# Modulation steps at equal distances, columns prepared a turn ahead and y summed in place in the mixer turns of a two-layer trunk

## The chip, the cores and the metric

The kernel runs on one core of a Trainium2 chip. The metric is the device time of one execution in microseconds (us); smaller is better. The core has TensorE (PE; its weight loads are shown apart as PEld), VectorE (DVE), ScalarE (ACT), GpSimd (POOL) and SyncE (SP), which issues most transfers.

## What is computed

The reference is one inference step of a diffusion trunk with two layers, for 512 latent and 128 context tokens of width 1024, in float32. The change lies in layer 0, whose mixer runs a state-space scan (16 heads, forwards and backwards) beside a gated convolution:

```python
def mixer_ssd_conv(h, P, e, h0):
    u = h @ P['ssd_w_in'][e]
    z, xbc, dt_raw, bg, cg, xin = jnp.split(u, [s1, s2, s3, s4, s5], axis=-1)
    y_a, states = ssd_mixer(z, xbc, dt_raw, ...)
    y_b = bg * dwconv(cg * xin, P['sc_conv_w'][e])
    return jnp.concatenate([y_a, y_b], axis=-1) @ P['mix0_w_out'][e], states

# in ssd_mixer, after the two scans:
    y = y_f + flip(y_b) + xs * jnp.sum(d_skip.astype(jnp.float32), axis=0)[:, None]
    y = y.reshape(b, l, SSD_INNER) * jax.nn.silu(z.astype(jnp.float32))

# in run_stream, for each layer:
    m = jax.nn.silu(cvec) @ P['ada_w'][i] + P['ada_b'][i]
```

The last line gives the modulation (shift, scale and gate of each of the 12 sections of 1024 columns). The kernel computes most of it during the mixer, section by section.

## The kernel before

Features lie on the 128 partitions, tokens along the free dimension: an activation chunk is 128 features by T = 644 columns (128 context, 4 of padding, 512 latent). Each float32 product is made of three: high by high, low by high and high by low, with weights split on the core. SyncE loads a weight block of 128 columns into `raw` (two buffers), ScalarE copies it to `w_hi` (`split`, L1092), GpSimd subtracts that from `raw` into `w_lo` (`low`, L550), and PE uses the pair from a ring of four slots.

The mixer makes eight turns, one for each pair of heads (j = 0 to 7), in two groups of four; `mixer_pair` holds PE's part of a turn. A turn has four products with weights (z, cg, xin, bg), each in two halves of four chunks (`gemm_half(s, h)`: lines L613, L614, L617, 24 products of 322 columns). The small products of the scan are written by hand between these halves: transposes of the pair's input `xsj`, rows of decays in bank 5 (`rows_of`), states, y and the context state. The second half of the last product and the first half of the next turn's first product stand at the turn's end, in that order. Engines meet by counting semaphores; every queue keeps the order of the program.

One turn also makes one modulation section in four steps (`section(0)` to `section(3)`, `ada_step`, L684: four products of 512 columns). Each step needs 1 MB of `ada_w` in the one buffer `ada`. SyncE may load a step only when PE has used the one before (`ada_used`), and SyncE's queue holds, in this order per turn: step 0, `raw` slots 0 and 1 of the next turn, step 1, slot 2, step 2, slot 3, step 3. A `raw` load waits until GpSimd has finished the slot two before it:

```python
sp.wait_ge(S["low_split"], b + s - RAW + 1 + 4 * i)     # weights(): a raw buffer is free
sp.wait_ge(S["ada_used"], step)                         # ada_load()
for s in ((0, 1), (2,), (3,), ())[q]: following(s)      # raw loads behind step q
```

On VectorE a turn begins with three copies: the pair's input to `xsj`, and the pair's columns of two tables to `pick` and `col` (L1706 to L1711); `prep_ready` then lets PE and ScalarE begin. It goes on with weighted inputs, differences of decays (`seg`, L1738), the states `hin` (L1756, waited for by PE before L844), the convolution (`gpad`, L1791; `cgs`, L1647 and L1648), y (L1797 to L1802: a sum into `xsj`, a product with the gate into `xs`), the second half of the mixer's output (`yb`, L1806) and, last, the modulation's columns (L1694), which it reads from the same bank 4 into which the next turn's transposes go. ScalarE makes exponentials, gates and splits; its order in a turn begins with the exponential of rows 0, that of `seg` 0, the gate `zs` of the finished first product, the exponential of rows 1 (`cs`, L1226), that of `seg` 1, and the split of the next turn's slot 0.

Of the kernel before, what the change touches and what calls it, by code (L numbers as in the profile page):

```python
# [20 lines left out]
ALU = mybir.AluOpType  # L21
ACT = mybir.ActivationFunctionType

P = 128
# [17 lines left out]
DR, DC = 15, 31  # L42
TABW = 64
BIG = 1e30
MIX_STEPS = 11
FF = 2816
FC = FF // P
FA = 12
# [81 lines left out]
def trunk(nc, x_prompt, x_sample, state_ssd, cache_k, cache_v, c, c_ctx, ada_w, ada_b, norm_mix_g, norm_ffn_g,  # L130
# [6 lines left out]
    with ExitStack() as ctx:  # L137
# [461 lines left out]
        def _(pe):  # L599
# [185 lines left out]
            def rows_of(u):  # L785

                lhs = pick[:, u % 2, u // 2:u // 2 + 1].broadcast_to([P, P])
                for b in range(2):
                    mm = t.matmul(ps[:, 5, 2 * b * P:2 * b * P + 2 * P], lhs, sum_rows[b][:], start=True, stop=True)
                mm.then_inc(S["rows_ready"], 1)  # L790

            def mixer_pair(j0, i, more=True):


                base = SLOT_MIX + 4 * j0

                def gemm_half(s, h, i=i):
                    if h == 0:
                        pe.wait_ge(S["low_split"], base + s + 1 + 4 * i)
                        tile_free(TILE_MIX + 4 * j0, 4, i, s)  # L800
                    mm = half_slot(s % 2, s % RING, range(4 * h, 4 * h + 4), act_hi, act_lo, h == 0, h == 1)
                    if h == 1:
                        mm.then_inc(S["slot_used"], 1)

                def section(q):

                    ada_step(7, ADA_STEPS * (j0 + i) + q, q)

                def bank5_free(n):
                    pe.wait_ge(S["seg_ready"], 5 * (j0 + i) + n)  # L810

                if i is None:
                    gemm_half(0, 0, 0)
                    return
                pe.wait_ge(S["prep_ready"], j0 + i + 1)
                for n in range(LC):
                    mm = t.transpose(ps[:, 4, n * P:n * P + P], xsj[:, LAT0 + n * P:LAT0 + n * P + P], ident[:])
                mm.then_inc(S["xtok_ready"], 1)
                rows_of(0)
                gemm_half(0, 1)  # L820
                section(0)
                bank5_free(1)
                rows_of(1)
                pe.wait_ge(S["xtok_taken"], j0 + i + 1)
                t.transpose(ps[:, 4, 0:P], xsj[:, 0:NCTX], ident[:])
                pe.wait_ge(S["h0_loaded"], 16 * (j0 + i) + 16)
                t.transpose(ps[:, 4, P:2 * P], h0[:, 0, :], ident[:])
                t.transpose(ps[:, 4, 2 * P:3 * P], h0[:, 1, :], ident[:]).then_inc(S["ctok_ready"], 1)
                gemm_half(1, 0)
                bank5_free(2)  # L830
                rows_of(2)

                pe.wait_ge(S["ctok_taken"], j0 + i + 1)
                for n in range(LC - 1):
                    mm = t.matmul(ps[:, 4, n * P:n * P + P], btok[:, n, :], xdw[:, 2, n, :], start=True, stop=True)
                mm.then_inc(S["hf_ready"], 1)
                gemm_half(1, 1)
                section(1)
                bank5_free(3)
                rows_of(3)  # L840

                pe.wait_ge(S["hf_taken"], j0 + i + 1)
                for n in range(LC - 1):
                    mm = t.matmul(ps[:, 4, n * P:n * P + P], btok[:, n + 1, :], xdw[:, 3, n + 1, :], start=True, stop=True)  # L844
                mm.then_inc(S["hb_ready"], 1)
                gemm_half(2, 0)
                bank5_free(4)

                for h in range(2):
                    for r in range(2):  # L850
                        lhs = col[:, LC * KINDS + K_DA, r, h:h + 1].broadcast_to([P, P])
                        mm = t.matmul(ps[:, 5, (2 * h + r) * P:(2 * h + r + 1) * P], lhs, tri[:, r, :], start=True, stop=True)
                mm.then_inc(S["rows_ready"], 1)
                gemm_half(2, 1)

                section(2)
                gemm_half(3, 0)
                section(3)

                pe.wait_ge(S["m_ready"], 3 * (j0 + i) + 2)  # L860
                pe.wait_ge(S["hb_taken"], j0 + i + 1)
                for n in range(LC):
                    cols = slice(n * P, n * P + P)
                    for r in range(4):
                        for h in range(2):
                            hc = slice(64 * h, 64 * h + 64)
                            lhs = xdw[:, r, n, hc] if r < 2 else hin[:, r - 2, n, hc]
                            rhs = mbuf[:, 2 * h + r, cols] if r < 2 else cs[:, 2 * h + r - 2, cols]
                            mm = t.matmul(ps[64 * h:64 * h + 64, 6, cols], lhs, rhs, start=(r == 0), stop=(r == 3))
                mm.then_inc(S["y_ready"], 1)  # L870
                pe.wait_ge(S["row_copied"], j0 + i + 1)
                ada_columns(4, 3 * P)

                pe.wait_ge(S["m_ready"], 3 * (j0 + i) + 3)
                for r in range(2):
                    t.matmul(ps[:, 4, r * P:r * P + P], xdw[:, 2 + r, LC, :], btok[:, LC, :], start=True, stop=True)
                for r in range(2):
                    for h in range(2):
                        mm = t.matmul(ps[64 * h:64 * h + 64, 4, 2 * P:3 * P], xdw[:, r, LC, 64 * h:64 * h + 64],
                                      mbuf[:, 4, (2 * h + r) * P:(2 * h + r + 1) * P], start=(r == 0), stop=(r == 1))  # L880
                mm.then_inc(S["cstate_ready"], 1)
                gemm_half(3, 1)
                if more:
                    gemm_half(0, 0, i + 1)
# [562 lines left out]
        def _(dve):  # L1447
# [242 lines left out]
            def modulation(m0, cols):  # L1690

                adab = par[:, bass.ds(R_ADAB + m0, C)].rearrange("p (b n) -> p b n", b=2).unsqueeze(3).broadcast_to([P, 2, C // 2, 2])
                dst = mod[:].rearrange("p m c s -> p (m c) s")[:, bass.ds(m0, C), :].rearrange("p (b n) s -> p b n s", b=2)
                tt(dst, cols.rearrange("p (n b s) -> p b n s", n=C // 2, b=2), adab, ALU.add).then_inc(S["mod_ready"], 1)  # L1694


            for g in range(GROUPS):
# [1 line left out]
                    group_taken(g)  # L1699
                j0 = (C // GROUPS) * g  # L1700
                tb = TILE_MIX + 4 * j0
                with st.loop(C // GROUPS, MIX_STEPS) as i:
                    j = j0 + i

                    st.wait()
                    st.did(v.tensor_copy(xsj[:], xs[:, bass.ds(j * T, T)]))  # L1706
                    mine = unit[:, bass.ds(2 * j, HEADS + 2)]
                    v.tensor_copy(pick[:], bass.AP(tensor=mine.tensor, offset=mine.offset, ap=[mine.ap[0], [HEADS, 2], [1, 2]]))
                    scv = sc[:].rearrange("p n k u -> p (n k u)")[:, bass.ds(2 * j, NC * KINDS * 32 - 14)]
                    pair = bass.AP(tensor=scv.tensor, offset=scv.offset, ap=[scv.ap[0], [32, NC * KINDS], [HEADS, 2], [1, 2]])  # L1710
                    v.tensor_copy(col[:], pair).then_inc(S["prep_ready"], 1)  # L1711
                    dve.wait_ge(S["prep_ready"], j + 1)
                    colv = col[:].rearrange("p (n k) r h -> p n k r h", k=KINDS)

# [69 lines left out]
                    for r in range(2):  # L1784
                        rl = slice(r * P, r * P + P)
                        ins = tt(m4[:, :, rl], m4[:, :, rl], bcast(gm[:, r, ctx_cols], 1, [P, 2, P]), ALU.mult)
                    ins.then_inc(S["m_ready"], 1)

                    dve.wait_ge(S["slot_used"], SLOT_MIX + 3 + 4 * j)
                    dve.wait_ge(S["tile_free1"], tb // 2 + 1 + 2 * i)  # L1790
# [3 lines left out]

                    dve.wait_ge(S["y_ready"], j + 1)
                    skip = dskip[:, bass.ds(j, 1)]
                    st.then_wait(stt(xsj[:, LAT0:T], xsj[:, LAT0:T], skip, ps[:, 6, :], ALU.mult, ALU.add))  # L1797
                    st.did(stt(xs[:, bass.ds(j * T + LAT0, NLAT)], xsj[:, LAT0:T], 0.5, zs[:, LAT0:T], ALU.mult, ALU.mult))
                    dve.wait_ge(S["cstate_ready"], j + 1)
                    v.tensor_copy(sto[:].rearrange("p r n -> p (r n)"), ps[:, 4, 0:2 * P]).then_inc(S["cstate_taken"], 1)  # L1800
                    st.then_wait(stt(xsj[:, 0:NCTX], xsj[:, 0:NCTX], skip, ps[:, 4, 2 * P:3 * P], ALU.mult, ALU.add))
                    st.did(stt(xs[:, bass.ds(j * T, NCTX)], xsj[:, 0:NCTX], 0.5, zs[:, 0:NCTX], ALU.mult, ALU.mult))  # L1802
                    st.wait()
                    dve.sem_inc(S["ya_ready"], 1)
                    dve.wait_ge(S["slot_used"], SLOT_MIX + 4 + 4 * j)
                    tt(F(yb[:, bass.ds(j * T, T)]), V(1), F(cgs[:]), ALU.mult).then_inc(S["tile_free1"], 1)  # L1806
                    add_squares(1, j)

                    dve.wait_ge(S["mod_turned"], j + 1)
                    modulation((2 + j) * C, ps[:, 4, 3 * P:3 * P + 2 * C])  # L1810

            inverse(1)
            with dve.Fori(0, C) as i:
# [280 lines left out]
```

## Time and profile before

| what | value |
|---|---|
| median of the runs shown | 2083.84 us (2082.85 to 2084.32, 3 runs) |
| the profiled execution | 2088.62 us |
| its span, first to last instruction | 2086.8 us |
| busy: PE, PEld, DVE, ACT, POOL | 94%, 90%, 50%, 33%, 31% of the span |
| mean granted clock of TensorE | 0.973 of full speed |
| the eight mixer turns | about 196 to 592 us of the span |

The busy share of PE is an average over stages; matmuls are pipelined and their ends are modelled, so 94% does not say that PE is at its peak for 94% of the time. Idle time of an engine matters only where another waits for it.

### The profile page before, as it was taken

The page shows a single profiled execution, that of the slowest core. Times are in us where ns is not written, and L with a number is a line of the kernel's source. Part 1 is how long each engine was busy: PE and PEld are TensorE (multiplying, and loading weights), DVE is VectorE, ACT ScalarE, POOL GpSimd, SP SyncE. Part 2 cuts the span into 40 slices and gives each one's busy share as a digit, 9 for nine tenths or more (in the row PEclk, how much of TensorE's full clock was granted, in tenths as well). Part 3 has the DMA queues.
Part 4 walks back from the last instruction along what each step waited for, and adds up shares of the span by engine and source line. Part 5 has one row for each costly group of instructions (what it writes and reads, how often), then busy time and mean ns, then how long its engine had stood idle before and what let it go on. Part 6 is the DMA issues. An engine that isn't in the chain of part 4 may idle for free. (4 is left out here: it accounts for less than half of the span.)

```text
span 2086.8 us, 36378 instructions
## 1 busy us (share of the span) xinstructions
PE 1971.2 (94%) x13563; PEld 1887.0 (90%) x13563; DVE 1042.2 (50%) x1987; ACT 687.4 (33%) x1043; POOL 637.7 (31%) x314
## 2 busy tenths in 40 slices
PE   6699999899999899999999988989999999999997
PEld 3498888787889899999999988989998999999997
DVE  3544776666661365521555334656635655125543
ACT  1433222222231244422323422127724434223333
POOL 0322222222223233344334522332212333433342
PEclk9899999999999999999999999999999999999998
DMA  8123444344444222223222341221031222232222
GB/s 290 41 58 89 145 145 144 120 135 148 129 166 145 81 64 71 70 69 90 71 70 57 97 136 52 71 56 29 19 132 43 80 80 58 75 89 70 65 64 73
DMA packets 280040, 192.31 MB, mean 92 GB/s; under 512 B 25370, under 2 KB 267414, under 8 KB 279462
## 3 DMA queue, kind: packets, MB, share of 16 engines
q1 hardware_dynamic: 276950, 185.61, 29.7%
q10 hardware_dynamic: 3024, 5.78, 0.7%
q8 instruction: 46, 0.75, 0.2%
q14 instruction: 20, 0.16, 0.0%
HBM read 181.31 MB, written 10.06 MB: 92 GB/s over the span
## 5 line engine op out<-in xcount | busy, mean ns | idle before, releaser
L550 POOL TENSOR_TENSOR w_lo<-raw,w_hi 128x1024 fp32r<-128x1024 f32 x244 | 591.7, 2426 | 1344.5 <-ACT w_hi L1092 1344.5
L613 PE MATMUL ps<-act_hi,w_hi 128*128 128x322 f32 x2752 | 850.6, 316 | 13.6 <-DVE act_lo L1554 11.6
L614 PE MATMUL ps<-act_lo,w_hi 128*128 128x322 f32 x2624 | 806.3, 313 | 0.0
L617 PE MATMUL ps<-act_hi,w_lo 128*128 128x322 f32 x2752 | 637.2, 313 | 0.0
L613 PEld LDWEIGHTS ps<-act_hi,w_hi 128*128 128x128 f32 x2752 | 528.2, 192 | 26.4 <-issue 16.4
L614 PEld LDWEIGHTS ps<-act_lo,w_hi 128*128 128x128 f32 x2624 | 501.4, 191 | 0.0
L617 PEld LDWEIGHTS ps<-act_hi,w_lo 128*128 128x128 f32 x2752 | 468.2, 190 | 0.0
L1092 ACT ACTIVATE w_hi<-raw 128x1024 fp32r<-128x1024 f32 x244 | 256.4, 1052 | 452.5 <-PE ps L617 400.0
L613 PE MATMUL ps<-f_hi,w_hi 128*128 128x322 f32 x704 | 214.2, 311 | 0.0
L614 PE MATMUL ps<-f_lo,w_hi 128*128 128x322 f32 x704 | 213.7, 310 | 0.0
L1827 DVE SCALAR_TENSOR_TENSOR x<-ps,mod,x 128x128 f32 (+1 forms) x144 | 54.4, 433 | 262.5 <-PE ps L617 262.0
L617 PE MATMUL ps<-f_hi,w_lo 128*128 128x322 f32 x704 | 161.9, 311 | 0.0
L613 PEld LDWEIGHTS ps<-f_hi,w_hi 128*128 128x128 f32 x704 | 133.5, 190 | 0.0
L614 PEld LDWEIGHTS ps<-f_lo,w_hi 128*128 128x128 f32 x704 | 132.8, 189 | 0.0
L1648 DVE SCALAR_TENSOR_TENSOR ft<-fg,par,ft 128x644 f32<-128x644 f32 x44 | 124.3, 2824 | 6.8 <-DVE ft L1647 6.5
L617 PEld LDWEIGHTS ps<-f_hi,w_lo 128*128 128x128 f32 x704 | 118.0, 188 | 0.0
L1863 DVE TENSOR_TENSOR fg<-ps,spread 128x644 f32<-128x644 f32 x44 | 36.5, 830 | 130.8 <-PE ps L617 122.1
L1339 ACT ACTIVATE fe<-ft,gb 128x130 f32<-128x130 f32 x88 | 44.9, 557 | 127.1 <-DVE ft L1648 127.1
L1482 DVE TENSOR_TENSOR acc<-acc,sq 128x644 f32<-128x644 f32 x48 | 65.6, 1367 | 28.1 <-ACT sq L1103 27.7
L1335 ACT ACTIVATE ft<-fg,par 128x644 f32<-128x644 f32 x44 | 36.7, 834 | 127.4 <-DVE fg L1863 127.3
L1647 DVE SCALAR_TENSOR_TENSOR ft<-fg,par,ft 128x644 f32<-128x644 f32 x44 | 43.3, 984 | 44.1 <-ACT ft L1335 43.6
L1343 ACT ACTIVATE f_hi<-fa 128x644 f32 x44 | 32.7, 743 | 95.1 <-DVE fa L1875 95.1
(294 smaller groups left out, 2173.2 us busy)
## 6 DMA issues: line engine op xcount, KB each, us to landing
ada<-in_ada_w SPq DMA_DIRECT2D x40, 1024.0 KB, 5.3
raw<-in_ssd_w_in SPq DMA_DIRECT2D x44, 512.0 KB, 3.9
raw<-in_ffn_w_gate SPq DMA_DIRECT2D x44, 512.0 KB, 3.8
raw<-in_ffn_w_up SPq DMA_DIRECT2D x44, 512.0 KB, 3.8
raw<-in_ffn_w_down SPq DMA_DIRECT2D x32, 384.0 KB, 3.4
raw<-in_na_w_qkv SPq DMA_DIRECT2D x24, 512.0 KB, 3.7
raw<-in_ffn_w_down SPq DMA_DIRECT2D x32, 320.0 KB, 3.2
first<-in_ada_w SPq DMA_DIRECT2D x8, 1024.0 KB, 12.1
```

Source lines behind the costliest of these rows:

```text
L550: g.tensor_tensor(w_lo[:, s], raw[:, s % RAW], w_hi[:, s], ALU.subtract).then_inc(S["low_split"], 1)
L613: t.matmul(out, hi, chunk_of(src_hi, k0 + k, cols), start=start, stop=False)
L614: t.matmul(out, hi, chunk_of(src_lo, k0 + k, cols), start=False, stop=False)
L617: mm = t.matmul(ps[:, 2 * tset + h, 0:HALF], lo, chunk_of(src_hi, k0 + k, cols), start=False, stop=stop)
L1092: a(w_hi[:, s], raw[:, s % RAW], ACT.Copy).then_inc(S["high_split"], 1)
L1335: a(ft[k][:], fg[k][:, 1:T + 1], ACT.Copy, scale=w1).then_inc(S["ffn_mid"], 1)
L1339: ins = a(fe[k][:, lo:hi], ft[k][:, lo:hi], ACT.Gelu_apprx_tanh, bias=gb[:, k, stream:stream + 1])
L1482: tt(acc[:], acc[:], sq[:], ALU.add).then_inc(S["squares_used"], 1)
L1647: st.then_wait(stt(dst[:], buf[:, 0:T], w[:, bass.ds(w0, 1)], dst[:], ALU.mult, ALU.add))
L1648: return stt(dst[:], buf[:, 2:T + 2], w[:, bass.ds(w2, 1)], dst[:], ALU.mult, ALU.add)
L1827: ins = stt(dst, ps[:, 2 * k + bank, lo:hi], gate, dst, ALU.mult, ALU.add)
L1863: tt(F(fg[k][:, 1:T + 1]), V(0), F(spread[:]), ALU.mult).then_inc(S["tile_free0"], 1)
```

## The change

There are five edits, all in the mixer's turns. PE's `section(0)`, `section(1)` and `section(2)` each move ahead of a half-product (sections 1 and 2 past further small products). VectorE's three copies become a function `prepare`, called once ahead of the first turn and then inside each turn, for the next one, just before the product into `gpad`; the last turn of the second group is written out behind its loop, without it. The modulation's columns move ahead of `yb`. PE waits for them (`mod_ready`) before the next turn's transposes, since VectorE no longer makes the copies behind them. y is summed and gated in `xs` itself, so that `xsj` is free early, and a step count goes from 11 to 10.

```diff
-MIX_STEPS = 11
+MIX_STEPS = 10
...
+                pe.wait_ge(S["mod_ready"], j0 + i + 1)
                 pe.wait_ge(S["prep_ready"], j0 + i + 1)
...
                 rows_of(0)
+                section(0)
                 gemm_half(0, 1)
-                section(0)
                 bank5_free(1)
...
                 gemm_half(1, 0)
+                section(1)
                 bank5_free(2)
...
                 gemm_half(1, 1)
-                section(1)
                 bank5_free(3)
...
                 gemm_half(2, 0)
+                section(2)
                 bank5_free(4)
...
                 gemm_half(2, 1)
-
-                section(2)
                 gemm_half(3, 0)
                 section(3)
...
-                    st.wait()
-                    st.did(v.tensor_copy(xsj[:], xs[:, bass.ds(j * T, T)]))
+                def prepare(j):
+
+                    if not (isinstance(j, int) and j == 0):
+                        dve.wait_ge(S["ctok_ready"], j)
+                    v.tensor_copy(xsj[:], xs[:, bass.ds(j * T, T)])
...
                     v.tensor_copy(col[:], pair).then_inc(S["prep_ready"], 1)
...
                     ins.then_inc(S["m_ready"], 1)
+                    if more:
+                        prepare(j + 1)
 
                     dve.wait_ge(S["slot_used"], SLOT_MIX + 3 + 4 * j)
...
-                    st.then_wait(stt(xsj[:, LAT0:T], xsj[:, LAT0:T], skip, ps[:, 6, :], ALU.mult, ALU.add))
+                    lat, ctx_ = xs[:, bass.ds(j * T + LAT0, NLAT)], xs[:, bass.ds(j * T, NCTX)]
+                    st.then_wait(stt(lat, lat, skip, ps[:, 6, :], ALU.mult, ALU.add))
+                    st.did(stt(lat, lat, 0.5, zs[:, LAT0:T], ALU.mult, ALU.mult))
...
                     dve.sem_inc(S["ya_ready"], 1)
+                    dve.wait_ge(S["mod_turned"], j + 1)
+                    modulation((2 + j) * C, ps[:, 4, 3 * P:3 * P + 2 * C])
                     dve.wait_ge(S["slot_used"], SLOT_MIX + 4 + 4 * j)
                     tt(F(yb[:, bass.ds(j * T, T)]), V(1), F(cgs[:]), ALU.mult).then_inc(S["tile_free1"], 1)
                     add_squares(1, j)
 
-                    dve.wait_ge(S["mod_turned"], j + 1)
-                    modulation((2 + j) * C, ps[:, 4, 3 * P:3 * P + 2 * C])
+                if g == 0:
+                    prepare(0)
+                loops = C // GROUPS - g
+                with st.loop(loops, MIX_STEPS) as i:
+                    pair_of_heads(i)
+                if g > 0:
+                    pair_of_heads(loops, more=False)
```

PE's order at the start of a turn, before and then after. `xsj` is the pair's input, `pick` the columns of `rows_of`, `ada` the modulation's weights, `act` and `w` the operands of a half-product.

```order
L817 MATMUL ps<-ident,xsj 128x128 x4
L789 MATMUL ps<-sum_rows_98,pick 128x256
L789 MATMUL ps<-sum_rows_99,pick 128x256
L613 MATMUL ps<-act_hi,w_hi 128x322
L614 MATMUL ps<-act_lo,w_hi 128x322
```
```order
L818 MATMUL ps<-ident,xsj 128x128 x4
L789 MATMUL ps<-sum_rows_98,pick 128x256
L789 MATMUL ps<-sum_rows_99,pick 128x256
L680 ISA
L684 MATMUL ps<-ada,csil_w 32x512 x4
L613 MATMUL ps<-act_hi,w_hi 128x322
L614 MATMUL ps<-act_lo,w_hi 128x322
```

The four products of section 0 (L684) now stand ahead of the half-product instead of behind it; its line of the transposes is L818 now.

PE's order at the end of `gemm_half(2, 0)`, before and then after. `tri,col` is the last product into bank 5.

```order
L617 MATMUL ps<-act_hi,w_lo 128x322 x2
L810 REGISTER_ALU
L852 MATMUL ps<-tri,col 128x128 x4
L613 MATMUL ps<-act_hi,w_hi 128x322
L614 MATMUL ps<-act_lo,w_hi 128x322
L613 MATMUL ps<-act_hi,w_hi 128x322
```
```order
L617 MATMUL ps<-act_hi,w_lo 128x322 x2
L680 ISA
L684 MATMUL ps<-ada,csil_w 32x512 x4
L810 REGISTER_ALU
L854 MATMUL ps<-tri,col 128x128 x4
L613 MATMUL ps<-act_hi,w_hi 128x322
L614 MATMUL ps<-act_lo,w_hi 128x322
L613 MATMUL ps<-act_hi,w_hi 128x322
```

Section 2 now stands ahead of the `tri` products; before, it stood behind them and the half-product that follows.

VectorE's order in mid-turn, before and then after: the last products of the decays (`mbuf`), then the product into `gpad`.

```order
L1786 TENSOR_TENSOR mbuf<-mbuf,gm 128x2x128 x2
L1789 REGISTER_ALU
L1790 REGISTER_ALU
L1791 TENSOR_TENSOR gpad<-ps,cgs 128x644
L1647 ISA
L1647 SCALAR_TENSOR_TENSOR cgs<-gpad,par,cgs 128x644
```
```order
L1789 TENSOR_TENSOR mbuf<-mbuf,gm 128x2x128 x2
L1706 ISA
L1706 COPY xsj<-xs 128x644
L1708 ISA
L1708 COPY pick<-unit 128x4
L1711 REGISTER_ALU
L1711 COPY col<-sc 128x100
L1794 REGISTER_ALU
L1795 ISA
L1796 TENSOR_TENSOR gpad<-ps,cgs 128x644
L1647 ISA
L1647 SCALAR_TENSOR_TENSOR cgs<-gpad,par,cgs 128x644
```

The three copies for the next turn now stand between the last product with `gm` and the product into `gpad`.

## Rows read from the trace of the kernel before

**Rows 1.** Waits of TensorE by line and releaser, window 196 to 592 us.

```profile
PE ps L684 <- DMA ada<-in_ada_w: 14.9, 8, 2.4
PE ps L817 <- DVE col L1711: 14.2, 8, 4.6
PE ps L844 <- DVE hin L1756: 2.2, 8, 0.3
```

**Rows 2.** Timeline of PE in one turn: start, length, line, operation, idle before.

```profile
247.97 0.66 PE L817 MATMUL ps<-ident,xsj 128*128 128x128 f32 x4 [0.97 <-DVE col L1711]
...
252.34 1.07 PE L684 MATMUL ps<-ada,csil_w 128*32 128x512 f32 x8
...
263.93 0.94 PE L844 MATMUL ps<-xdw,btok 128*128 128x128 f32 x6 [0.28 <-DVE hin L1756]
...
268.26 1.05 PE L852 MATMUL ps<-tri,col 128*128 128x128 f32 x8
...
272.80 1.07 PE L684 MATMUL ps<-ada,csil_w 128*32 128x512 f32 x8
...
279.41 1.06 PE L684 MATMUL ps<-ada,csil_w 128*32 128x512 f32 x8 [1.81 <-DMA ada<-in_ada_w]
...
280.41 0.66 PE L869 MATMUL ps<-mbuf,xdw 128*64 128x128 f32 x8
...
294.54 0.66 PE L817 MATMUL ps<-ident,xsj 128*128 128x128 f32 x4 [0.97 <-DVE col L1711]
```

**Rows 3.** Busy time by stretch and engine, granted clock (third from the end).

```profile
326.00:332.50 6.50, 6.42 (x73) 5.41 (x74) 0.00 (x0) 0.60 (x1) 0.00 (x0) 0.74 0.62 196
521.00:527.00 6.00, 6.00 (x72) 5.14 (x64) 0.00 (x0) 0.60 (x1) 0.00 (x0) 0.72 0.63 203
569.00:575.50 6.50, 5.82 (x66) 4.31 (x68) 0.00 (x0) 0.60 (x1) 0.00 (x0) 0.74 0.44 141
```

**Rows 4.** Timeline of SyncE's queue, 172 to 300 us.

```profile
177.05 7.51 SPq L353 DMA_DIRECT2D raw<-in_ssd_w_in  x2
184.60 0.58 SPq L418 DMA_DIRECT2D ada<-in_ada_w  x1
...
260.32 0.37 SPq L353 DMA_DIRECT2D raw<-in_ssd_w_in  x1
...
274.07 0.37 SPq L418 DMA_DIRECT2D ada<-in_ada_w  x1
```

**Rows 5.** The page's DMA issues: count, KB each, median us to landing.

```profile
ada<-in_ada_w SPq DMA_DIRECT2D x40, 1024.0 KB, 5.3
raw<-in_ssd_w_in SPq DMA_DIRECT2D x44, 512.0 KB, 3.9
```

**Rows 6.** The tile `ada`, issues from 184 to 186 us (one).

```profile
DMA to landing us min/median/max: 6.1/6.1/6.1
```

**Rows 7.** Timeline of ACT in the same turn as rows 2.

```profile
253.08 0.69 ACT L1236 ACTIVATE zs<-ps 128x644 f32<-128x644 f32 x1
253.88 0.60 ACT L1226 ACTIVATE cs<-ps 128x512 f32<-128x512 f32 x1
```

**Rows 8.** Timeline of PE: first turn of each of the two groups.

```profile
198.97 1.12 PE L817 MATMUL ps<-ident,xsj 128*128 128x128 f32 x4 [4.60 <-DVE col L1711]
...
393.84 1.11 PE L817 MATMUL ps<-ident,xsj 128*128 128x128 f32 x4 [3.74 <-DVE col L1711]
```

**Rows 9.** Timeline of DVE: the turn of rows 2, then the group change.

```profile
273.00 0.83 DVE L1791 TENSOR_TENSOR gpad<-ps,cgs 128x644 f32<-128x644 f32 x1 [0.66 <-PE ps L617]
...
284.33 0.75 DVE L1797 SCALAR_TENSOR_TENSOR xsj<-xsj,dskip,ps 128x512 f32<-128x512 f32 x1 [5.43 <-PE ps L869]
...
291.69 2.60 DVE L1706 COPY xsj<-xs 128x644 f32 x1
...
392.98 0.50 DVE L1706 COPY xsj<-xs 128x644 f32 x1 [0.35 <-DVE btok L1673]
```

**Rows 10.** Timeline of POOL, 285 to 296 us.

```profile
291.18 2.77 POOL L550 TENSOR_TENSOR w_lo<-raw,w_hi 128x1024 fp32r<-128x1024 f32 x1 [12.96 <-ACT w_hi L1092]
```

More of the change, by code:

```diff
@@ L1701, in _ @@
                 tb = TILE_MIX + 4 * j0
-                with st.loop(C // GROUPS, MIX_STEPS) as i:
-                    j = j0 + i
-                    st.wait()
-                    st.did(v.tensor_copy(xsj[:], xs[:, bass.ds(j * T, T)]))
+                def prepare(j):
+                    if not (isinstance(j, int) and j == 0):
+                        dve.wait_ge(S["ctok_ready"], j)
+                    v.tensor_copy(xsj[:], xs[:, bass.ds(j * T, T)])
                     mine = unit[:, bass.ds(2 * j, HEADS + 2)]
@@ L1711, in _, with pair_of_heads @@
                     v.tensor_copy(col[:], pair).then_inc(S["prep_ready"], 1)
+                def pair_of_heads(i, more=True):
+                    j = j0 + i
                     dve.wait_ge(S["prep_ready"], j + 1)
@@ L1796, in _ @@
                     skip = dskip[:, bass.ds(j, 1)]
-                    st.then_wait(stt(xsj[:, LAT0:T], xsj[:, LAT0:T], skip, ps[:, 6, :], ALU.mult, ALU.add))
-                    st.did(stt(xs[:, bass.ds(j * T + LAT0, NLAT)], xsj[:, LAT0:T], 0.5, zs[:, LAT0:T], ALU.mult, ALU.mult))
+                    lat, ctx_ = xs[:, bass.ds(j * T + LAT0, NLAT)], xs[:, bass.ds(j * T, NCTX)]
+                    st.then_wait(stt(lat, lat, skip, ps[:, 6, :], ALU.mult, ALU.add))
+                    st.did(stt(lat, lat, 0.5, zs[:, LAT0:T], ALU.mult, ALU.mult))
                     dve.wait_ge(S["cstate_ready"], j + 1)
                     v.tensor_copy(sto[:].rearrange("p r n -> p (r n)"), ps[:, 4, 0:2 * P]).then_inc(S["cstate_taken"], 1)
-                    st.then_wait(stt(xsj[:, 0:NCTX], xsj[:, 0:NCTX], skip, ps[:, 4, 2 * P:3 * P], ALU.mult, ALU.add))
-                    st.did(stt(xs[:, bass.ds(j * T, NCTX)], xsj[:, 0:NCTX], 0.5, zs[:, 0:NCTX], ALU.mult, ALU.mult))
+                    st.then_wait(stt(ctx_, ctx_, skip, ps[:, 4, 2 * P:3 * P], ALU.mult, ALU.add))
+                    st.did(stt(ctx_, ctx_, 0.5, zs[:, 0:NCTX], ALU.mult, ALU.mult))
                     st.wait()
                     dve.sem_inc(S["ya_ready"], 1)
+                    dve.wait_ge(S["mod_turned"], j + 1)
+                    modulation((2 + j) * C, ps[:, 4, 3 * P:3 * P + 2 * C])
                     dve.wait_ge(S["slot_used"], SLOT_MIX + 4 + 4 * j)
```

## Prediction

> **What bounds the kernel now.** I read the waits of TensorE first, over the eight mixer turns (196 to 592 us of a span of 2086.8). Two waits matter: 14.9 us in eight pieces for the transfer into `ada`, and 14.2 us in eight pieces for `col`, the last copy that VectorE makes ahead of a turn; a third, 2.2 us for `hin`, is small [rows 1]. Then the timeline of one turn, PE alone, shows where they stand. A turn begins with the transposes of `xsj` (I call that moment T0, here 247.97). Its four modulation sections (L684) start at 252.34, one not shown, 272.80 and 279.41: the last two are 6.6 us apart, and the fourth stands 1.81 us idle. After the y product and two half-products the next transposes stand 0.97 us idle [rows 2]. Outside these, PE goes from one product to the next, so in these turns PE is the bound and each of its idle stretches is on the path.
>
> Third, the granted clock. In the turn of rows 2 y ran at full clock (its first eight products take 0.66 us); so it did in four others. In three of the eight turns the stretch around y shows a granted clock of 0.74, 0.72 and 0.74 [rows 3], a mix of the levels 2.4 and 1.2 GHz. Ahead of y PE had in every turn stood idle for the `ada` wait, 2.4 us in the longest [rows 1]. The loss is 6.5 x 0.26 + 6.0 x 0.28 + 6.5 x 0.26 = 5.1 us.
>
> The profiled execution took 2088.62 us, of which 2086.8 is the span; that is 4.8 above the median of the runs, 2083.84. I make the sum against the profiled execution and take the same difference off the median. About 0.2% of it, 4 us, is what a measurement can tell from no change.
>
> **Sections moved up.** Sections 0, 1 and 2 each change places with a half-product. A half takes 3.5 to 3.8 us: 272.80 - 268.26 less 1.05 for the `tri` products gives 3.5, and 279.41 - 1.81 - 272.80 less 1.00 for the section's own products (279.41 to 280.41) gives 3.8 [rows 2]. After the change at least two halves lie between any section and the next, so sections start 8 us or more apart (1.0 + 2 x 3.5). What must fit between them: the section's own 1.0, the SyncE issue 0.2 behind its last product (272.80 + 1.07 to 274.07 [rows 2, 4]), and 5.3 us to land [rows 5]: 6.5 us. So the wait before section 3 goes: -14.9 us. PE does the same products as before.
>
> The tight place is section 2. SyncE's queue issues the load for it behind `raw` of slot 2 of the next turn, and that issue waits for GpSimd's low part, not for PE: 260.32, which is T0 + 12.35 [rows 4]. Section 2 will stand where the `tri` products stand now, T0 + 20.29 [rows 2]. In the one place where an `ada` load stood right behind a `raw` load (the second of the pair at 177.05 ends at 184.56 and is issued 0.37 before that, `ada` at 184.60), it landed after 6.1 us instead of 5.3 [rows 4 to 6]. So it is issued at T0 + 12.8 to 13.2 and lands at 18.9 to 19.3: 1.0 to 1.4 us to spare, and I cost this wait at 0. The bound from the other side lets the two transfers pass one after the other whole: 12.35 + 3.9 + 5.3 = 21.55 [rows 5], 1.3 us too late, 8 x 1.3 = 10 us.
>
> A rule of the Trainium skill speaks for that bound: the page DMA: Bandwidth & Descriptors, section Queues, rings and completion order, says that each DMA engine takes the descriptors of one ring in order, so `ada` stands behind the whole `raw` load. The trace agrees that it is later, by 0.8 us and not by the 3.9 of a whole load; by the page's order alone with whole loads the gain would be 10 us less.
>
> **ScalarE behind section 0.** ScalarE's gate (`zs`) needs the first product whole, and that now ends 1.0 us later. Today `zs` runs at 253.08, when the product has been done since 252.34, and the exponential of the second rows (`cs`) follows at 253.88 [rows 7]. With the product's end at about 253.4, `zs` starts at about 253.5 and `cs` at about 254.2, 0.3 later. VectorE's chain to `hin` hangs on `cs`, and PE waits for `hin` already (0.28 [rows 2]), so this is on the path: +0.3 x 8 = 2.4 us. Bounds: 0, and the whole of section 0, 8 us. SyncE's issue and section 2 both shift by it, so the margin above stays.
>
> **Columns prepared in mid-turn.** The copies to `xsj`, `pick` and `col` go to the place before the `gpad` product. Six of the eight starts lose 0.97 each: -5.8. The first start, 4.60, keeps its wait: the copies still follow the last input block there. At the change of groups, 3.74, PE also waits for the new scores; only the copies go, with 0.35 of idle time ahead: 393.84 - 392.98 + 0.35 = 1.2 [rows 8, 9]. Together -7.0 us. After the change the new scores (`btok`) are what is late there.
>
> What the copies cost at the new place: 0.50 us for the large one when GpSimd is idle (392.98), 2.60 when GpSimd runs its low part (291.18 to 293.95, and the copy ends at 294.29 [rows 9, 10]). GpSimd's low part of slot 2 starts only behind `gpad` (its split follows ScalarE's scaling of `gpad`), and that of slot 1 is by then done, so I take 0.9 for the three. VectorE idles 0.66 there now and section 2 delays both it and PE alike, so `gpad` comes at most 0.3 late. Cover behind it: VectorE idles 5.43 us before y [rows 9], of which 1.81 (the removed wait) and 1.0 (section 2 ahead of it) go, and 2.6 is left. Even the 2.60 copy would fit; without the cover the modulation would come late, and PE needs that only at the next turn, two halves later. So: 0.
>
> **Modulation ahead of `yb`, y in place.** PE's new wait at a turn's start is for the modulation, and PE's whole turn is queued behind it, so every engine would wait with it. Its products are done before PE begins the last two halves (7 us), and VectorE has it right behind y, so this wait is 0. y in place changes operands, not counts: 0. The extra copy of the last turn's code runs straight on: 0.
>
> **Clock.** With no idle stretch before y, I take the three drops as gone: -5.1. Bounds: 0 if they stay, 3.4 more gain or loss if the slow stretch behind each of the two long starts (198.97, 393.84 [rows 8]) ends one turn's worth (1.7, as each drop above) earlier or later.
>
> **Sum.** -14.9 - 5.8 - 1.2 - 5.1 + 2.4 = -24.6. Profiled execution 2064.0, runs 2083.84 - 24.6 = 2059.2.
>
> **Rivals.**
> The wait goes to section 2. For: the load is issued late by GpSimd's pace and meets `raw`. Against: 6.1 us, not 9. It costs 0 to 10 us, at most 2069. Chance 0.15.
> The clock drops stay, as the narrow y products follow section 3 as before. For: they happen in y. Against: five turns with the same y had none. 2064.3. Chance 0.15.
> The change doesn't do what it says: section 3 still waits, since its load is queued behind `raw` of slot 3. Against: that is issued before section 2 ends. Only the turn starts gain: 2083.84 - 7.0 + 2.4 = 2079.2. Chance 0.05.
> Slower. The place is the same load of section 2: SyncE can't issue it before GpSimd's low part of the next turn's slot 0, which waits for ScalarE's split behind `cs`. If that chain slipped as section 0 moved, each turn would wait at section 2. It decides against the change above 24.6 / 8 = 3.1 us a turn, which is an issue at T0 + 12.8 + 1.2 + 3.1 = 17 instead of 12.8; at 4 us a turn the time would be 2059.2 + 32 = 2091. Nothing in ScalarE's order puts it there. Chance 0.05.
>
> **Numbers.** The forecast has 0.60. Its own range, from the ScalarE term at 0 and earlier clock (2059.2 - 2.4 - 3.4 = 2053.4) to that term at 0.7 a turn (+3), is 2053.4 to 2062. To leave out no more than 2 in 10 the range reaches over the first two rivals, whose bound is 2069: 2053 to 2069; the third rival and the slower one lie above it (0.10), the rest is left for what lies below. Faster by over 0.2% (below 2079.7): forecast, first two rivals and half of the third, 0.92; within 0.2%: 0.03; slower 0.05.
>
> **What would show it.** PE's waits in the mixer: nothing or little for `ada`, at turn starts only the first (4.6) and the one at the group change (about 2.5), `hin` about 4.6 in eight pieces. The granted clock 1.0 in all stretches of y. Turns about 44 us instead of the 46.6 of rows 2 (294.54 - 247.97). SyncE's `ada` issue about 13 us behind T0, PE at section 2 without idle. The prediction is wrong if PE idles at section 1 or 2, if `hin` costs more than 1 us a turn, or if VectorE's copy takes 2.6 and `gpad` delays PE.

## The result, and the profile after

The changed kernel takes 2060.06 us (median of 4 runs, 2059.49 to 2061.25), the kernel before 2084.08 (4 runs, 2082.85 to 2085.19): a ratio of 0.9886, 95% interval 0.9868 to 0.9903, or 24.0 us less. The forecast was 2059.2, with 24.6 us less. The profiled execution took 2059.84 us (span 2057.8), 28.8 less than that of before; its mean granted clock is 0.977, that of before 0.973. One run of the kernel before (3227.25 us at a granted clock of 0.56) and one of the experiment with section 2 a half earlier (2358.16 us at 0.77) lie far above all others and are left out of the ratios and averages below.

The waits of TensorE in the mixer turns: the waiting line, what released it, us in total, how many times, the longest one.

```profile
PE ps L845 <- DVE hin L1759: 5.0, 8, 0.6
PE ps L818 <- DVE col L1711: 4.6, 1, 4.6
PE ps L818 <- DVE btok L1673: 2.9, 1, 2.9
```

Against [rows 1]: the line for `ada` is gone, 14.9 us. The waits at the turn starts (L817 before, L818 now) fall from 14.2 to 4.6 + 2.9 = 7.5. The wait for `hin` (L844 before, L845 now) grows from 2.2 to 5.0. These three are -14.9 - 6.7 + 2.8 = -18.8 us.

PE in one turn, the one that answers to [rows 2]:

```profile
245.20 0.60 PE L818 MATMUL ps<-ident,xsj 128*128 128x128 f32 x4
...
245.97 1.06 PE L684 MATMUL ps<-ada,csil_w 128*32 128x512 f32 x8
...
254.85 1.06 PE L684 MATMUL ps<-ada,csil_w 128*32 128x512 f32 x8
...
261.47 0.71 PE L845 MATMUL ps<-xdw,btok 128*128 128x128 f32 x4 [0.64 <-DVE hin L1759]
...
265.87 1.07 PE L684 MATMUL ps<-ada,csil_w 128*32 128x512 f32 x8
...
275.09 1.06 PE L684 MATMUL ps<-ada,csil_w 128*32 128x512 f32 x8
...
276.08 0.66 PE L869 MATMUL ps<-mbuf,xdw 128*64 128x128 f32 x8
...
289.09 0.60 PE L818 MATMUL ps<-ident,xsj 128*128 128x128 f32 x4
```

The four sections start at 245.97, 254.85, 265.87 and 275.09, 8.9 to 11.0 us apart, and none waits. The next transposes follow without idle time. The turn takes 289.09 - 245.20 = 43.9 us (46.6 before). The first eight products of y take 0.66 us.

The granted clock (third number from the end) from 6 us into the first turn to the end of the last; the middle line is the change of groups:

```profile
206.00:381.00 175.00, 170.20 (x1355) 151.96 (x1354) 118.96 (x293) 49.87 (x70) 41.84 (x16) 1.00 0.46 148
381.00:388.00 7.00, 6.38 (x46) 5.43 (x47) 4.05 (x14) 1.95 (x4) 0.00 (x0) 1.00 0.47 149
388.00:555.00 167.00, 163.33 (x1304) 145.07 (x1302) 113.71 (x285) 49.21 (x69) 39.58 (x16) 1.00 0.46 147
```

No stretch of y falls below full clock; [rows 3] had three with 0.72 to 0.74. The two long starts, which answer to [rows 8]:

```profile
199.75 1.09 PE L818 MATMUL ps<-ident,xsj 128*128 128x128 f32 x4 [4.59 <-DVE col L1711]
...
381.62 0.63 PE L818 MATMUL ps<-ident,xsj 128*128 128x128 f32 x4 [2.86 <-DVE btok L1673]
```

At the change of groups PE waits 2.86 us instead of 3.74, now for `btok`, and the four transposes behind it take 0.63 us instead of 1.11: this time they ran at 2.4 GHz.

Of the 28.8 us between the two profiled executions, 18.8 are waits. The other 10.0 are the clock for the most part: 5.1 in the three stretches of [rows 3], and up to 5 at the two long starts. Here are 7 us around each of them before, then around the first of them now; the second one now is the middle line above.

```profile
197.80:204.80 7.00, 5.83 (x23) 5.83 (x24) 4.89 (x15) 1.23 (x2) 0.58 (x1) 0.51 0.28 75
...
392.40:399.40 7.00, 5.56 (x23) 5.56 (x24) 4.81 (x17) 1.12 (x2) 0.00 (x0) 0.51 0.00 1
```

```profile
199.50:206.50 7.00, 6.75 (x37) 4.90 (x38) 3.88 (x13) 1.23 (x2) 0.00 (x0) 0.76 0.59 163
```

That is 7 x (0.49 + 0.49 - 0.24) = 5.2 us, less what PE idled there in any case.

Of the 24.0 us between the medians, the same waits leave 5.2, and only about half of that is the clock. The profiled execution of before lay 4.5 us above its median, that of after at its own. For every run the span and the mean granted clock are on record, and span x (1 - clock) is the most that the run can have lost to the lower clock (a step of 0.001 is 2 us, so only averages count). It is 56 us in the profiled execution of before, but 51.0 on average over the 35 runs of that kernel beside the experiments, and 48.4 over ten runs of the changed kernel (four here, six in the repeat below). So between typical runs the clock gives about 2.6 us, give or take 1.6. Most of the rest fits another reading: a wait costs a little more than the idle time listed for it. Both turns shown ran at full clock; they differ by 46.57 - 43.89 = 2.7 us, while their waits differ by 1.81 + 0.97 - 0.36 = 2.4, which makes about 2 us in eight turns.

### The profile page after: what moved, and what is told of

Its sections match the earlier page's. It is cut to its first block and busy times, and to the rows that moved or that the text cites. A ratio compares the mean times of both kernels' runs of the same rounds, so it can differ in the third digit from the quotient of the medians.

```text
span 2057.8 us, 36345 instructions
## 1 busy us (share of the span) xinstructions
PE 1960.3 (95%) x13563; PEld 1879.5 (91%) x13563; DVE 1026.1 (50%) x1987; ACT 687.6 (33%) x1043; POOL 637.8 (31%) x314
## 5 line engine op out<-in xcount | busy, mean ns | idle before, releaser
L613 PEld LDWEIGHTS ps<-act_hi,w_hi 128*128 128x128 f32 x2752 | 526.8, 191 | 27.3 <-issue 17.2
```

The source lines that it names most:

```text
L613: t.matmul(out, hi, chunk_of(src_hi, k0 + k, cols), start=start, stop=False)
```

## The experiments

Each run is compared with the kernel before on its own chip; those medians were 2083.8 to 2084.3. The edit of the first experiment is shown against the kernel before, that of the queue order against the run ahead of it, the others against the changed kernel. For scale, the changed kernel once more:

> The changed kernel itself, on the chip of the two others, for comparison: 2060.

It took 2060.15 us (ratio 0.989, 0.9871 to 0.9909). In its profile the change of groups ran at the lower clock again (1.00 in the execution above), although the kernel is the same:

```profile
381.00:388.00 7.00, 6.15 (x25) 4.29 (x26) 4.28 (x14) 1.23 (x2) 0.00 (x0) 0.51 0.21 49
```

So a part of the 5 us at the long starts is chance of the execution.

**Sections alone.** PE's three sections move up, VectorE's part stays as before.

```diff
                 rows_of(0)
+                section(0)
                 gemm_half(0, 1)
-                section(0)
...
                 gemm_half(2, 0)
+                section(2)
...
                 gemm_half(2, 1)
-                section(2)
```

> Only PE's sections 0, 1 and 2 move up; VectorE keeps its old order. Theory of the prediction: the eight waits for ada (14.9 us) go, hin rises from 2.2 to about 5 us, the turn starts keep their 14.2 us, and y runs at full clock in every turn: 14.9 + about 5 - 2.8 = 17 us less than before, about 2067. Rival (the clock in y has nothing to do with the idle stretch ahead of it): the drops stay, 12 us less, about 2072. Rival (an earlier section finds its load late): ada waits show at section 1 or 2 and the gain is under 10 us.

Measured: 2069.26 us, ratio 0.9931 (0.9915 to 0.9947), 15.0 us less than before. PE's waits, then the granted clock before and after the change of groups:

```profile
PE ps L817 <- DVE col L1710: 14.2, 8, 4.6
...
PE ps L844 <- DVE hin L1755: 5.1, 8, 0.6
```

```profile
206.00:386.00 180.00, 170.95 (x1356) 151.95 (x1354) 125.22 (x294) 49.88 (x70) 41.85 (x16) 1.00 0.47 144
392.00:560.00 168.00, 162.51 (x1298) 143.74 (x1297) 119.56 (x280) 48.06 (x68) 39.10 (x15) 1.00 0.48 148
```

The line for `ada` is gone, `col` is untouched and `hin` rises by 2.9: both waits change where the prediction said and by its sizes. No stretch of y falls below full clock, against the rival. Waits alone give 12.0, so 3 us are left for the clock, between the theory's 5 and the rival's 0. The granted clocks of the runs say the same: span x (1 - clock) is 46.9 us on average here and 50.0 for the kernel before on this chip.

**Columns alone.** All of VectorE's part, with the sections at their old places.

```diff
-                section(0)
                 gemm_half(0, 1)
+                section(0)
...
-                section(2)
...
                 gemm_half(2, 1)
+                section(2)
```

> Only VectorE's part (columns prepared in mid-turn, modulation ahead of yb, y in place); PE's sections stay where they were before. Theory of the prediction: col waits fall from 14.2 to about 7.5 us, ada stays at 14.9, hin at 2.2, and some of the clock drops in y stay: 7 us less than before, about 2077, and granted clock under 1.0 around y in some turns. Rival (the turn starts only hand their wait on to section 3): about 2084. Rival (drops in y go with the columns): about 2072.

Measured: 2074.81 us, ratio 0.9963 (0.9949 to 0.9977), 9.4 less. PE's waits, then the granted clock before and after the change of groups:

```profile
PE ps L684 <- DMA ada<-in_ada_w: 14.5, 8, 2.2
PE ps L818 <- DVE col L1711: 4.6, 1, 4.6
PE ps L818 <- DVE btok L1673: 2.9, 1, 2.9
PE ps L845 <- DVE hin L1759: 2.2, 8, 0.3
```

```profile
202.00:385.00 183.00, 171.91 (x1367) 152.21 (x1366) 119.26 (x294) 49.74 (x70) 42.15 (x16) 1.00 0.48 143
390.00:566.00 176.00, 166.04 (x1323) 146.28 (x1321) 114.10 (x285) 50.11 (x72) 40.33 (x16) 1.00 0.48 146
```

The turn starts gain as worked out (`col` and `btok` 7.5 us, as in the changed kernel). In the profiled execution the clock stayed at 1.00 in all stretches of y, although PE stood idle 14.5 us in eight pieces ahead of them. So that idle time doesn't bring a drop each time. But this execution (2072.06 us) is the fastest of eight, which reach to 2078.19, and its granted clock of 0.977 is the highest: span x (1 - clock) is 47.6 us in it and 51.6 on average, against 50.0 for the kernel before on this chip. So over the runs the columns alone show no gain on the clock, as the first theory says, while the sections alone show 3 us; the median lies between the first theory's 2077 and the third's 2072.

**One step back.** Section 2 alone returns to its old place in the changed kernel.

```diff
                 gemm_half(2, 0)
-                section(2)
...
                 gemm_half(2, 1)
+                section(2)
                 gemm_half(3, 0)
```

> The changed kernel, with section 2 alone back at its old place, 6.6 us ahead of section 3. Theory of the prediction: section 2's move alone carries the gain on ada: 1.8 us a turn come back ahead of section 3, 14.5 us, and none, some or all of the 5 us of clock drops: 2074.5 to 2080. Rival (the moves of sections 0 and 1 carry part of it): less than 8 us of ada waits, under 2068.

Measured: 2075.48 us, ratio 0.996 (0.9946 to 0.9973).

```profile
PE ps L684 <- DMA ada<-in_ada_w: 14.3, 8, 2.4
```

The move of section 2 alone carries the gain on `ada`; the moves of sections 0 and 1 carry nothing of it. In the profile the clock fell in y in one of the eight turns (0.57 from 325.9 to 329.9 us).

**Section 2 a half earlier.** It stands ahead of `gemm_half(2, 0)`.

```diff
+                section(2)
                 gemm_half(2, 0)
-                section(2)
```

> The changed kernel, with section 2 one half-product earlier still (ahead of gemm_half(2, 0)), so that PE comes for its load before it can have landed and the wait shows when that is. Theory of the prediction: the load, issued 13.3 us into the turn behind raw, lands after 5.6 to 6.1 us, and PE comes at about 17.0: a wait of 1.9 to 2.4 us a turn on L684, 15 to 19 us more than the changed kernel, about 2075 to 2079 (more if the clock falls). Rival (the two loads pass one after the other whole, landing at 21.7): 4.7 us a turn, about 2097. Rival (no wait even here): 2060.

Measured: 2089.2 us, ratio 1.0023 (1.0011 to 1.0035): slower than before. Section 2 in the first two turns, the granted clock in the turns of either group, and the landing of the load issued at 262.09:

```profile
220.69 1.94 PE L684 MATMUL ps<-ada,csil_w 128*32 128x512 f32 x8 [2.04 <-DMA ada<-in_ada_w]
...
268.11 1.93 PE L684 MATMUL ps<-ada,csil_w 128*32 128x512 f32 x8 [2.09 <-DMA ada<-in_ada_w]
```

```profile
206.00:396.00 190.00, 176.39 (x1357) 154.87 (x1355) 118.81 (x293) 49.87 (x70) 41.63 (x16) 0.96 0.44 136
402.00:586.00 184.00, 172.44 (x1324) 153.92 (x1322) 113.44 (x285) 50.03 (x71) 39.35 (x15) 0.96 0.43 138
```

```profile
DMA to landing us min/median/max: 6.0/6.0/6.0
```

The load lands after 6.0 us, and PE waits 1.9 to 2.5 us a turn, 17.2 us over the eight turns: the landing of the prediction, not the serial one. What the expectation left open is the clock. It fell in each of the eight turns: in the first group the eight products of the section take 1.93 or 1.94 us instead of 1.07, in the second 1.06 to 1.33, and there the drop comes behind them. The time is 29 us above the changed kernel, of which 17 are waits.

**The same with another queue order.** SyncE holds the load for section 2 ahead of `raw` of slot 2.

```diff
-                    for s in ((0, 1), (2,), (3,), ())[q]:
+                    for s in ((0, 1), (), (2, 3), ())[q]:
```

> The kernel of the run section2_early, with one more edit: SyncE's queue holds the load for section 2 ahead of raw of slot 2 instead of behind it. Theory: in section2_early the load was late only because it stood behind raw in the queue, which waits for GpSimd; issued when section 1 is done (about 11 us into the turn), it lands at about 16.5, ahead of PE at 17.0. The 17 us of waits and the clock drops behind them go: about 2060. Rival (1 MB can't land between sections so close, whatever the order): 1 us or more a turn stays, over 2070.

Measured: 2063.08 us, ratio 0.9892 (0.9869 to 0.9915), with no wait for `ada` in the profile. So the time at which the load for section 2 lands, and with it the margin at section 2, is set by the queue, as the prediction had it: the load is issued when GpSimd has freed `raw`, not when PE has freed `ada`.

**A larger dose.** Section 2 right ahead of section 3, so that a whole load's time is idle ahead of y.

```diff
-                section(2)
...
                 gemm_half(3, 0)
+                section(2)
                 section(3)
```

> The changed kernel, with section 2 right ahead of section 3, so that PE stands idle for a whole load (about 5.4 us) ahead of y in each turn: a larger dose of what the prediction blames for the drops of the clock in y. Idle time alone: 8 x 5.4 = 43 us more, about 2103. Theory (idle time ahead of y brings the drops): y runs at 1.2 GHz in part in nearly every turn, 1.7 to 3.4 us each, 2117 to 2130. Rival (the drops come from y or from chance): the clock in y is as in the changed kernel, 2103.

Measured: 2121.35 us, ratio 1.0176 (1.0161 to 1.0192). The waits of PE for `ada`, and the first turn's section 3 with the y product behind it:

```profile
PE ps L684 <- DMA ada<-in_ada_w: 43.9, 8, 5.9
```

```profile
236.77 1.93 PE L684 MATMUL ps<-ada,csil_w 128*32 128x512 f32 x8 [5.37 <-DMA ada<-in_ada_w]
...
238.64 1.12 PE L869 MATMUL ps<-mbuf,xdw 128*64 128x128 f32 x8
```

43.9 us are idle; the time rose by 61 us above the changed kernel, so 17 are left for the clock, in the range of the theory. Section 3 takes 1.93 us and the first eight products of y 1.12 (1.06 and 0.66 in the changed kernel).

**The gate.** ScalarE's gate behind the exponential of rows 1.

```diff
-                    main_used(0)
-                    a(F(zs[:]), V(0), ACT.Tanh, scale=0.5).then_inc(S["gate_tanh"], 1)
                     rows_exp(1)
+                    main_used(0)
+                    a(F(zs[:]), V(0), ACT.Tanh, scale=0.5).then_inc(S["gate_tanh"], 1)
```

> The changed kernel, with ScalarE's gate (zs) behind the exponential of rows 1 instead of ahead of it. Theory of the prediction: the gate, which waits for the first product behind section 0, is what makes the states late; without it hin falls from 0.64 to about 0.3 a turn, 2.5 us less than the changed kernel, about 2057.5. Rival (hin is late for another reason, such as VectorE's own order): 5.0 us of hin and 2060 stay.

Measured: 2059.55 us, ratio 0.9875 (0.9852 to 0.9898).

```profile
PE ps L845 <- DVE hin L1759: 2.1, 8, 0.3
```

The wait is back at 2.1 us, so the gate is what made the states late. The median shows nothing of the 2.9 us and lies nearer to the rival's time, but it can't decide: the six runs reach from 2048.91 to 2061.37. In the two profiled executions the clock took the gain, at the change of groups and at the mixer's end. First this run, then the same stretches of the changed kernel:

```profile
377.00:387.00 10.00, 7.14 (x40) 5.06 (x39) 6.25 (x18) 1.23 (x2) 0.00 (x0) 0.83 0.43 125
552.00:564.00 12.00, 9.64 (x50) 9.31 (x49) 8.58 (x14) 8.53 (x14) 2.63 (x1) 0.72 0.73 265
```

```profile
377.60:387.60 10.00, 7.14 (x55) 5.96 (x53) 6.25 (x18) 1.55 (x3) 0.00 (x0) 1.00 0.48 143
552.40:564.40 12.00, 9.64 (x59) 9.31 (x58) 8.27 (x13) 8.57 (x15) 2.64 (x1) 0.86 0.71 262
```

10 us at 0.83 and 12 at 0.72, against 1.00 and 0.86, make 1.7 + 1.7 = 3.4 us.

**States ahead of the first decays.** VectorE's products of decays 0 go behind the states.

```diff
-                    decayed(0)
                     dve.wait_ge(S["gate_tanh"], j + 1)
...
                     states(0)
+                    decayed(0)
                     decayed(1).then_inc(S["m_ready"], 1)
```

> The changed kernel, with VectorE's products of decays 0 (one of which takes 2.87 us beside GpSimd's low part) moved behind the states: gate, seg 2, states 0, then decays 0 and 1. Theory: the wait for hin is on the path, so all of it goes, 5 us less than the changed kernel, about 2055. Rival (PE's idle time there is covered or comes back at rows 3 or at gpad): 2060, with as much idle time on another line.

Measured: 2052.63 us, ratio 0.9856 (0.9835 to 0.9877). All that is left of PE's waits in the turns, then the starts of two turns:

```profile
PE ps L818 <- DVE col L1711: 4.6, 1, 4.6
PE ps L818 <- DVE btok L1673: 2.9, 1, 2.9
```

```profile
241.77 0.60 PE L818 MATMUL ps<-ident,xsj 128*128 128x128 f32 x4
...
284.78 0.60 PE L818 MATMUL ps<-ident,xsj 128*128 128x128 f32 x4
```

No wait for `hin` is left, and none took its place: it was on the path. The time is 7.5 us below the changed kernel, where 5 were expected. The turn takes 43.0 us instead of 43.9, so a wait listed with 0.64 us cost 0.9, 7 us in eight turns.

**The modulation.** Its columns go back behind `yb`.

```diff
-                    modulation((2 + j) * C, ps[:, 4, 3 * P:3 * P + 2 * C])
...
                     add_squares(1, j)
+                    modulation((2 + j) * C, ps[:, 4, 3 * P:3 * P + 2 * C])
```

> The changed kernel, with the modulation's columns back behind yb and its squares. Theory of the prediction: PE needs them only at the next turn, behind a half-product, so nothing moves: 2060, and no wait on mod at the turn starts. Rival (the place ahead of yb is what lets PE start at once): a wait on mod at seven turn starts, up to 1 us each, 2062 to 2067.

Measured: 2063.64 us, ratio 0.9896 (0.9878 to 0.9914). The time lies in the rival's range, but the runs (2059.97 to 2065.45) overlap with those of the changed kernel on the same chip (2058.85 to 2065.01). No wait of PE for the modulation shows at a turn's start, so the rival's mechanism falls. At the mixer's end the wait for `roots` (L662) is 1.2 us instead of 0.6; whether the place is worth more than that can't be told from these times.

**The second group's scores earlier.** With states first, PE makes them ahead of the next turn's first half-product.

```diff
                 gemm_half(3, 1)
+                if ahead is not None:
+                    ahead()
                 if more:
                     gemm_half(0, 0, i + 1)
...
+            mixer_pair(0, C // GROUPS - 1, ahead=second_scores)
```

> The kernel of the run states_first, and the scores of the second group (group_scores(1), with its wait for the modulation) ahead of the first half-product of the next turn instead of behind it; the last turn of group 0 is written out on PE. Theory: what is late at the change of groups is VectorE's copy of the scores, 2.9 us, and 3.65 us of products cover it: 2.9 us less than states_first, and up to 1.7 more where the clock fell there, 2048 to 2050. Rival (PE then waits at the scores for the modulation instead): 2052 to 2053.

Measured: 2049.97 us, ratio 0.9837 (0.9824 to 0.9851): faster than both kernels.

```profile
PE ps L818 <- DVE col L1716: 4.6, 1, 4.6
```

This is PE's only wait left in the turns. The 2.9 us at the change of groups are gone.

## Why the prediction was right

Each term for a wait held, with its mechanism. The term for the clock was about twice what typical runs show, and that the sum still came within 0.6 us of the 24.0 is in part luck.

**Sections.** The eight waits for `ada` went, 14.9 us, and came back with section 2 alone (14.3 us, 2075.48).

**The tight place.** The prediction had the load issued 12.8 to 13.2 us into the turn and landing at 18.9 to 19.3. SyncE in the turn shown above, and the landing of its `ada` load:

```profile
257.86 0.37 SPq L353 DMA_DIRECT2D raw<-in_ssd_w_in  x1
...
258.48 0.39 SPq L418 DMA_DIRECT2D ada<-in_ada_w  x1
```

```profile
DMA to landing us min/median/max: 5.6/5.6/5.6
```

Issued at 258.48 - 245.20 = 13.3, landed at 18.9, and PE comes at 20.7: 1.8 us to spare. The run with section 2 a half earlier used that up and waited 1.9 to 2.5. A whole `raw` load ahead costs 0.3 to 0.7 us here (5.6 and 6.0 against 5.3), not 3.9. The rule of the Trainium skill that spoke for a serial landing (DMA: Bandwidth & Descriptors, section Queues, rings and completion order), that each DMA engine takes the descriptors of one ring in order, is not contradicted: `raw` landed after 3.7 us, at 261.6, and `ada` at 264.1.

The prediction overlooked a tighter place, section 1. Its load follows the second `raw` load of the pair by 1.3 us:

```profile
247.23 0.37 SPq L418 DMA_DIRECT2D ada<-in_ada_w  x1
```

```profile
DMA to landing us min/median/max: 6.5/6.5/6.5
```

It lands at 253.7, and PE comes at 254.85: 1.1 us to spare. In the next two turns it lands after 6.9 and 6.7 us and leaves 0.7 and 0.9. The prediction took 5.3 there; this cost nothing.

**ScalarE.** 0.3 a turn were forecast, 0.36 measured (0.64 - 0.28), by the chain that was named:

```profile
250.84 0.71 ACT L1236 ACTIVATE zs<-ps 128x644 f32<-128x644 f32 x1 [0.48 <-PE ps L617]
251.44 0.59 ACT L1226 ACTIVATE cs<-ps 128x512 f32<-128x512 f32 x1
```

The gate waits for the first product, and `cs` follows at 251.44, 6.24 us into the turn (5.91 before, [rows 7] less T0). Putting the gate behind `cs` took the added wait away again.

**Columns.** -5.8 and -1.2 were forecast; the long starts came out as 4.59 and 2.86 (4.6 and about 2.5 forecast), -6.7 in all. VectorE in mid-turn and at y:

```profile
270.98 0.49 DVE L1706 COPY xsj<-xs 128x644 f32 x1
...
271.74 0.83 DVE L1796 TENSOR_TENSOR gpad<-ps,cgs 128x644 f32<-128x644 f32 x1
...
280.05 0.75 DVE L1803 SCALAR_TENSOR_TENSOR xs<-xs,dskip,ps 128x512 f32 x1 [2.43 <-PE ps L869]
```

The copy takes 0.49, as with GpSimd idle, `gpad` follows 0.76 behind its start without idle time, and VectorE still stands 2.43 us ahead of y (2.6 forecast).

**Clock.** The reason held in the main, the size did not. The 5.1 us were read from one execution of the kernel before, which lost up to 56 us to the clock where 35 others lost up to 51.0 on average; between typical runs about 2.6 went. About 2 us that the waits cost beyond their listed idle time made up for the rest. That idle time ahead of y makes drops there possible is shown. The executions of before, columns alone and section 2 back, with 1.5 to 2.4 us idle ahead of y, had a drop in y in 3, 0 and 1 of their eight turns. The eight profiled executions without a wait for `ada` had none in 64 turns, and the larger dose had one in each turn. That 1.8 us of it brings them was too simple, and the length of the wait alone doesn't decide: drops stood behind waits of 1.83, 1.91 and twice 2.38 us, and none behind one of 2.16. What decides, turn by turn, stays open. The clock at the long starts, which the prediction kept at 0 with 3.4 us either way, gave up to 5 between the two profiled executions, partly by chance.

## What to carry to other kernels

Where one buffer is reloaded between uses, space the uses by the time from the last reader to the landing, and look at what stands ahead of that load in its queue: here the margins were 0.7 to 1.8 us, and one of them hung on a transfer that waits for another engine. When work moves up on the bound engine, look at what moves down with it: a product that ended 1.0 us later added 2.8 us of waits through a gate in another engine's queue, and re-ordering that engine took them away. Judge gains of a few microseconds by the waits in the profile as well as by the time, since the clock can take as much. And take a loss by the clock from the granted clocks of many runs: one profiled execution is one sample.

## What was not expected

With section 2 a half early, the clock fell in every turn, so that a wait of 2.1 us a turn cost 3.6 (29 us over eight turns). With waits of similar length right ahead of y it fell in 4 of 24 profiled turns. Whether what follows the wait, the length of the turn or something else makes the difference was not tested.
